# Stationary rows of a transformer kernel: high and low values, and in places the two token halves, stored interleaved

## The chip, the cores and the metric

The kernel runs on one core of one Trainium2 chip. The metric is the device time of one execution in microseconds (us), the median of the runs made. The core's engines are TensorE (in the profile PE for its matmuls and PEld for its weight loads), VectorE (DVE), ScalarE (ACT), GpSimd (POOL) and SyncE (SP, which issues most DMAs).

## What is computed

Two transformer layers on 256 tokens of width 1024, all in float32. The first has a gated delta rule and an HGRN2 mixer, then an MLP; the second has convolutions, then a layer of 16384 experts. The two places that the change touches are the MLP's down product (`y` below) and the product of the expert layer's gated activations with the table `v`:

```python
u = jnp.einsum('btd,df->btf', rms_norm(h, pre_mlp_norm[i]), w_mlp_up[i])
y = jnp.einsum('btf,fd->btd', jnp.square(jax.nn.relu(u)), w_mlp_down[i])
...
u_sel = jnp.take(u, idx, axis=0)
act = jax.nn.gelu(jnp.einsum("chkd,cd->chk", u_sel, xc))
v_sel = jnp.take(v, idx, axis=0)
return jnp.einsum("chk,chkd->cd", act * gates, v_sel)
```

The kernel doesn't gather rows of the experts. It multiplies all tokens with all 16384 rows of `u`, weights the result with a gate matrix that is zero where an expert wasn't picked, and multiplies all of that with all rows of `v`.

## The kernel before

**Precision.** A float32 product is made as three products in the fast format `float32r`: each operand is split into a high part (a copy rounded to float32r, made by ACT) and a low part (the float32 value less its high part, made by DVE), and high times high, low times high and high times low are added up in PSUM.

**Stages.** Weights stream in tiles of 128 partitions x 1024 float32 (512 KB) through `ring`, 4 slots deep. ACT splits off `w_hi` (line 1336), DVE `w_lo` (line 1988; GpSimd does it in the expert stage's first half), each 2 slots deep. The order of work is written out by hand on each engine, with semaphores between them.

There are two ways to use a tile on TensorE. In a column product (`up_block` and `out_block`) the weight tile is stationary and 256 tokens move. In a **row product** (`row_tile`, through `passes` at line 639; `closing_rows` at lines 711 and 716 for the last two tiles of a stage) the tokens are stationary and the weights move: for each of the two token halves `t` and the two column halves `c`, 128 token values per partition are loaded and 512 weight columns are streamed. One tile is 12 such pairs of load and matmul: 4 high times high, 4 low times high, then 4 high times low.

**MLP down product** (some 204 to 378 us, between the up products): four rounds, each of 8 tiles up and 8 tiles down. The stationary rows are `mid_hi` and `mid_lo`, 8 buffers `m` of 256 token values each. ACT writes the high part (`mid_copy`, line 1520), DVE the low one (`mid_low`, line 2270). Of the last round the two last tiles go through `closing_rows`.

**Last expert product** (966 us to the end): 128 blocks `n` of 128 experts. 94 are plain tiles, 92 of them through `row_tile` and the last 2 through `closing_rows`. The other 34 form 17 pairs (`pair_products`, lines 1225, 1226 and 1229): two blocks are multiplied as a 2 x 2 block product in 7 products in place of 8, with sums of weights and sums of rows made by DVE. A pair starts at an even `n`; three of its seven products use rows of `wgt` (one of the even block, two of the odd), and four use `pair_x`. The stationary rows `wgt_hi` and `wgt_lo` have 2 buffers, `j % 2`, written by `wgt_high` (line 1730, and line 1783 in the loop) on ACT and by `wgt_low` (line 2651) on DVE. In this stage DVE also splits the weights and makes the sums and low parts of the pairs (lines 2671 and 2676).

In both places the 256 values of a high or low part lie side by side, tokens 0 to 127 first, so one weight load reads 128 consecutive float32, 512 bytes:

```python
wgt_hi = sb("wgt_hi", [P, 2, T], F32R)
wgt_lo = sb("wgt_lo", [P, 2, T], F32R)
mid_hi, mid_lo = split_area("mid", 8, T)
...
return wgt_hi[:, j % 2, t * P:(t + 1) * P], wgt_lo[:, j % 2, t * P:(t + 1) * P]
```

Two further stationary operands serve the prediction. `open_sums` (line 985) clears four PSUM banks by matmuls of bfloat16 zeros with 512 columns. And in the mixer's output product and the gate product the stationary rows come from `hT`, whose block `k` starts at a multiple of 1088 bytes: `out_lhs` takes block `OUT_ORDER[j]` (4, 5, 6, 7, 0, 1, 2, 3) at byte 1088 k, and `gate_lhs` takes block k at byte 1088 k + 64.

Of the kernel before, what the change touches and what calls it, by code (L numbers as in the profile page):

```python
# [17 lines left out]
NT = T // P  # L18
# [41 lines left out]
PEER_BODY = 4  # L60
# [82 lines left out]
def two_stack_kernel(nc, x_in, pT_in, consts_in, cols_in, rows_in, small_in, wab_in, meta_in,  # L143
                     keys_in, stream_in, out):
    ctx = ExitStack()
    with ctx:
        def sb(name, shape, dt=F32):
            return ctx.enter_context(nc.sbuf_tensor(name, shape, dt))
# [22 lines left out]
        hotg = consts[:, C_TRI + 768:C_TRI + 1792].bitcast(F16).rearrange("p (a i n e) -> p a i n e", a=2, i=2, n=4)  # L171
        part16 = consts[:, C_TRI + 256:C_TRI + 384].bitcast(F16)
        sb("up_to_line", [P, (arena_at - nc.sbuf_base) % 512 // 4])
        wgt_hi = sb("wgt_hi", [P, 2, T], F32R)
        wgt_lo = sb("wgt_lo", [P, 2, T], F32R)
        metaT = sb("metaT", [P, KD, META])
        def groups_until(e):

# [4 lines left out]
        taken = [0]  # L183
# [75 lines left out]

        taken[0] = taken_shared  # L260
        mid = area(2, T)
        mid_hi, mid_lo = split_area("mid", 8, T)
        up = area(2, T)
        post = area(NT, D)
        emb = area(NT, D)
# [313 lines left out]
        def _(pe):  # L579
# [408 lines left out]
            transposes(2)  # L988
            open_sums()

            def mid_lhs(m, t):
                return mid_hi[:, m, t * P:(t + 1) * P], mid_lo[:, m, t * P:(t + 1) * P]

            def up_tile(i, m):

# [218 lines left out]


            def wgt_lhs(j, t):
                return wgt_hi[:, j % 2, t * P:(t + 1) * P], wgt_lo[:, j % 2, t * P:(t + 1) * P]

            def pair_products(k):

                n0, first, last = PAIRS[k], k == 0, k == len(PAIRS) - 1

                def high(b, x, w):

                    nc.tensor.matmul(bank[b][:, :], x[0], w, start=first and b >= 4, stop=False)  # L1225
                    nc.tensor.matmul(bank[b][:, :], x[1], w, start=False, stop=False)  # L1226

                def low(b, x, w):
                    return nc.tensor.matmul(bank[b][:, :], x[0], w, start=False, stop=last and b >= 4)  # L1229

                def rows_part(j, t):
                    o = slice(t * P, (t + 1) * P)
                    return wgt_hi[:, (n0 + j) % 2, o], wgt_lo[:, (n0 + j) % 2, o]
# [45 lines left out]
        def _(act):  # L1279
# [235 lines left out]
            def mlp_round(i, closing):  # L1515

                def mid_copy(m):

                    act.wait_ge(mid_step, i * 8 + m + 1)
                    nc.scalar.activation(mid_hi[:, m, :], mid[:, m % 2, :], ACT.Copy).then_inc(mid_high, 1)  # L1520

                for m in range(8):
                    hi(G_MLP + m + S, i, 16)
# [203 lines left out]

            def wgt_high(j, at):

                nc.scalar.activation(wgt_hi[:, j % 2, :], act_all[:, at, :], ACT.Copy).then_inc(wgt_step, 1)  # L1730

            for e in range(TAIL, N_KEYS):
                gelu_turn(e)
# [45 lines left out]
            with act.Fori(0, V_LOOPED) as i:  # L1779
                for j in range(PEER_BODY):  # L1780
                    hi(G_V + j + S, i, PEER_BODY)
                    act.wait_ge(tiles_done, i * PEER_BODY + (G_V + j + 1))
                    nc.scalar.activation(wgt_hi[:, j % 2, :],
                                         act_all[:, bass.ds(i * PEER_BODY + (j + 2), 1), :].rearrange("p a t -> p (a t)"),
                                         ACT.Copy).then_inc(wgt_step, 1)
            for n in range(V_LOOPED * PEER_BODY + 2, N_KEYS):
                if n in G_OF and n - 2 not in PAIR_OF:
# [165 lines left out]
        def _(dve):  # L1953
# [313 lines left out]
            def mid_low(i, m):  # L2267

                dve.wait_ge(mid_high, i * 8 + (mid_high0 + m + 1))
                nc.vector.tensor_tensor(mid_lo[:, m, :], mid[:, m % 2, :], mid_hi[:, m, :].bitcast(F32),  # L2270
                                        ALU.subtract).then_inc(mid_out, 1)

            def mlp_round(i, closing):
# [374 lines left out]
            def wgt_low(j, at, n):  # L2648

                dve.wait_ge(wgt_step, n + 1)  # L2650
                nc.vector.tensor_tensor(wgt_lo[:, j % 2, :], at, wgt_hi[:, j % 2, :].bitcast(F32), ALU.subtract)\  # L2651
                    .then_inc(wgt_out, 1)

            for e in range(TAIL, N_KEYS):
# [269 lines left out]
```

## Time and profile before

| | before |
|---|---|
| median of 2 runs | 1313.28 us (1312.39 to 1314.16) |
| the profiled execution | 1312.56 us, of which its span 1310.8 us |
| PE busy | 1283.9 us, 98% of the span, 7580 matmuls |
| PEld busy (weight loads) | 1121.9 us, 86% |
| DVE busy | 1029.5 us, 79% |
| ACT busy | 808.8 us, 62% |
| POOL busy | 441.3 us, 34% |
| chain that ended last | PE 84%, DVE 11% |
| row products in that chain (L639 with column products) | 41% of the span |

The chain that ended last is followed back from the last instruction. The end of a matmul in the profile is modelled: a matmul of 512 columns shows as 389 ns, while the next one starts after 227 ns. So the pace of a stream of matmuls is read from the starts, not from the durations; where several are merged in the view in order of time, the distance between two merged rows' starts over the count is their pace.

### The profile page before, as it was taken

What the parts mean: (1) busy time and instruction counts of PE and PEld (TensorE: products, weight loads), DVE (VectorE), ACT (ScalarE), POOL (GpSimd) and SP (SyncE); (2) the same over time, 40 slices, a digit from 0 to 9 for tenths busy, and PEclk for the clock granted to TensorE, in tenths of its full rate; (3) what the DMA queues carried; (4) which work ended last, traced back from release to release, by engine and by line L of the source; (5) the groups of instructions that cost most, each with busy time, mean ns of one, the idle gap of its engine ahead of it and who ended that gap; (6) DMA issues with size and microseconds to landing.
All of it is one profiled execution on the core that took longest, in us unless ns stands there. A gap on an engine that the chain in (4) does not pass through costs nothing.

```text
span 1310.8 us, 22781 instructions
## 1 busy us (share of the span) xinstructions
PE 1283.9 (98%) x7580; PEld 1121.9 (86%) x7580; DVE 1029.5 (79%) x2015; ACT 808.8 (62%) x1553; POOL 441.3 (34%) x255
## 2 busy tenths in 40 slices
PE   7999999999998999999999999999999999999997
PEld 7998988888877997998888888888888888888886
DVE  4787658556666985689996889898746899999996
ACT  6546446445566445455667888888756566666664
POOL 2100415000023754038888777777750000000000
PEclk9999999999999999999999999999999999999999
DMA  8533136565544544545555455444466665655553
GB/s 306 178 113 112 35 97 202 192 192 191 188 163 142 169 131 129 175 162 188 183 185 181 161 162 161 162 162 162 161 196 223 223 203 199 204 197 193 196 190 113
DMA packets 64651, 225.38 MB, mean 172 GB/s; under 512 B 7200, under 2 KB 7712, under 8 KB 64176
## 3 DMA queue, kind: packets, MB, share of 16 engines
q1 hardware_dynamic: 62832, 218.36, 50.6%
q10 hardware_dynamic: 1728, 5.84, 1.3%
q8 instruction: 53, 0.87, 0.3%
q14 instruction: 38, 0.31, 0.1%
HBM read 223.12 MB, written 1.05 MB: 171 GB/s over the span
## 4 chain that ended last, share of the span: by engine, by line
PE 84%; DVE 11%; issue 2%; ACT 1%; DMA 0%; POOL 0%; SPq 0%; POOLq 0%; ACTq 0%; DVEq 0%
PE bank L639 41%; PE bank L654 17%; PE bank L659 9%; PE bank L1198 2%; PE bank L1225 2%; PE bank L1226 2%; PE bank L1229 2%; DVE arena L2521 1%; DVE arena L2524 1%; DVE arena L2523 1%; DVE bank L2503 1%; DVE w_lo L1988 1%; DVE arena L2522 1%; PE bank L755 1%; PE bank L903 1%
## 5 line engine op out<-in xcount | busy, mean ns | idle before, releaser
L1336 ACT ACTIVATE w_hi<-ring 128x1024 fp32r<-128x1024 f32 x380 | 402.1, 1058 | 340.3 <-issue 167.2
L1988 DVE TENSOR_TENSOR w_lo<-ring,w_hi 128x1024 fp32r<-128x1024 f32 x225 | 275.3, 1224 | 141.1 <-ACT w_hi L1336 140.2
L1940 POOL TENSOR_TENSOR w_lo<-ring,w_hi 128x1024 fp32r<-128x1024 f32 x128 | 308.2, 2409 | 142.0 <-ACT w_hi L1336 142.0
L654 PE MATMUL bank<-hT,w_hi 128*128 128x512 f32 x1272 | 324.1, 396 | 1.9 <-ACT arena L1678 1.9
L654 PEld LDWEIGHTS bank<-hT,w_hi 128*128 128x128 f32 x1272 | 228.2, 189 | 43.2 <-ACT arena L1678 2.3
L1837 POOL TENSOR_SCALAR mstat<-mstat 128x1 f32<-128x1 f32 x16 | 5.8, 362 | 536.1 <-ACT bank L1293 334.2
L659 PEld LDWEIGHTS bank<-hT,w_lo 128*128 128x128 f32 x1272 | 173.5, 190 | 12.7
L659 PE MATMUL bank<-hT,w_lo 128*128 128x256 f32 x1272 | 177.1, 282 | 0.0
L639 PE MATMUL bank<-w_hi,wgt_hi 128*128 128x512 f32 x368 | 143.4, 390 | 0.2 <-DVE wgt_lo L2651 0.2
L639 PE MATMUL bank<-w_hi,wgt_lo 128*128 128x512 f32 x368 | 143.2, 389 | 0.0
L639 PE MATMUL bank<-hT,w_hi 128*128 128x256 f32 (+2 forms) x848 | 113.1, 286 | 0.0
L639 PEld LDWEIGHTS bank<-hT,w_hi 128*128 128x128 f32 x848 | 106.1, 189 | 0.6
L639 PE MATMUL bank<-w_lo,wgt_hi 128*128 128x512 f32 x368 | 98.4, 389 | 0.0
L2503 DVE TENSOR_TENSOR bank<-bank,consts 128x256 f32<-128x256 f32 x128 | 55.0, 432 | 48.0 <-ACT consts L1656 40.6
L1730 ACT ACTIVATE wgt_hi<-arena 128x256 fp32r<-128x256 f32 x116 | 47.0, 406 | 63.6 <-PE bank L639 60.5
L639 PEld LDWEIGHTS bank<-w_hi,wgt_hi 128*128 128x128 f32 x368 | 69.1, 188 | 15.2 <-issue 1.0
L1718 ACT ACTIVATE consts<-consts,idxT 128x128 f16<-128x128 f16 x256 | 81.4, 396 | 0.0
L639 PEld LDWEIGHTS bank<-w_lo,wgt_hi 128*128 128x128 f32 x368 | 69.1, 188 | 14.4
L639 PEld LDWEIGHTS bank<-w_hi,wgt_lo 128*128 128x128 f32 x368 | 69.1, 188 | 14.2
L1901 POOL TENSOR_TENSOR w_lo<-ring,w_hi 128x1024 fp32r<-128x1024 f32 x26 | 62.8, 2414 | 25.9 <-ACT w_hi L1336 24.5
L639 PE MATMUL bank<-hT,w_lo 128*128 128x256 f32 (+2 forms) x424 | 59.4, 282 | 0.0
L2651 DVE TENSOR_TENSOR wgt_lo<-arena,wgt_hi 128x256 fp32r<-128x256 f32 x128 | 54.7, 428 | 5.1 <-ACT wgt_hi L1730 5.1
(397 smaller groups left out, 2190.1 us busy)
## 6 DMA issues: line engine op xcount, KB each, us to landing
ring<-in_stream SPq DMA_DIRECT2D x380, 512.0 KB, 3.6
arena<-in_stream SPq DMA_DIRECT2D x34, 512.0 KB, 4.6
arena<-in_rows ACTq DMA_DIRECT2D x1, 1536.0 KB, 11.3
consts<-in_consts ACTq DMA_DIRECT2D x1, 1152.0 KB, 6.8
arena<-in_keys ACTq DMA_DIRECT2D x1, 1024.0 KB, 4.7
h<-in_x SPq DMA_DIRECT2D x2, 256.0 KB, 4.0
h<-in_x ACTq DMA_DIRECT2D x2, 256.0 KB, 3.9
arena<-in_rows ACTq DMA_DIRECT2D x1, 512.0 KB, 4.1
```

The lines of the kernel that those rows point to most:

```text
L639: mm = nc.tensor.matmul(o, a, b, start=first and not low_part and xp is x[0], stop=last and low_part)
L654: mm = nc.tensor.matmul(both, w_hi[:, slot, k * P:(k + 1) * P], x_both[:, k, :, :], start=k == 0, stop=False)
L659: mm = nc.tensor.matmul(bank[b][:, 0:T], w_lo[:, slot, k * P:(k + 1) * P], x_hi[:, k, :], start=False, stop=k == KD - 1)
L1198: mm = nc.tensor.matmul(bank[half][:, n * P:(n + 1) * P], hot2[:, half, n, :], hotg[:, half, i, n, :], start=i == 0, stop=i == 1)
L1336: nc.scalar.activation(w_hi[:, g % S, :], ring[:, g % R, :], ACT.Copy).then_inc(hi_done, 1)
L1718: ins = nc.scalar.activation(hotg[:, s % 2, 0, n, :], hot1[:, n, :], ACT.Copy, scale=idxT[:, 2, 4 * s + n:4 * s + n + 1])
L1730: nc.scalar.activation(wgt_hi[:, j % 2, :], act_all[:, at, :], ACT.Copy).then_inc(wgt_step, 1)
L1901: nc.gpsimd.tensor_tensor(w_lo[:, g % S, :], ring[:, g % R, :], w_hi[:, g % S, :].bitcast(F32), ALU.subtract).then_inc(lo_done, 1)
L1940: nc.gpsimd.tensor_tensor(w_lo[:, g % S, :], ring[:, g % R, :], w_hi[:, g % S, :].bitcast(F32), ALU.subtract).then_inc(lo_done, 1)
L1988: nc.vector.tensor_tensor(w_lo[:, g % S, :], ring[:, g % R, :], w_hi[:, g % S, :].bitcast(F32), ALU.subtract).then_inc(lo_done, 1)
L2503: nc.vector.tensor_tensor(half, half, up_u[:, at % 2, :], ALU.add).then_inc(up_out, 1)
L2651: nc.vector.tensor_tensor(wgt_lo[:, j % 2, :], at, wgt_hi[:, j % 2, :].bitcast(F32), ALU.subtract)\
```

## The change

The high and the low rows of one buffer now share 512 values, in one of five layouts. In each, the load of one part of one token half still reads 128 values; what differs is the step from one to the next. `apart` is the old layout (step 4 bytes). `by_part` interleaves high with low (step 8). `by_token` interleaves the token halves and keeps high and low apart (step 8). `by_all` interleaves both (step 16). `by_two` interleaves two neighbouring buffers as well (step 32).

- `wgt`: even buffer `by_part`, odd buffer `by_all`.
- `mid`: buffers 0 and 1 `by_part`, 2 `by_all`, 3 `by_token`, 4 and 5 `by_two`, 6 and 7 `apart`.

The writes on ACT and DVE get the same step, by the same instructions. No instruction, no wait and no matmul is added, removed or moved on any engine, and the buffers take the same bytes as before.

```diff
-        wgt_hi = sb("wgt_hi", [P, 2, T], F32R)
-        wgt_lo = sb("wgt_lo", [P, 2, T], F32R)
+        wgt_both = sb("wgt_both", [P, 2, 2 * T], F32R)
+        def apart(buf):
+            return [buf[:, n * T:(n + 1) * T].rearrange("p (t n) -> p t n", t=NT) for n in range(2)]
+        def by_part(buf):
+            both = buf.rearrange("p (t n a) -> p a t n", t=NT, a=2)
+            return [both[:, n, :, :] for n in range(2)]
+        def by_token(buf):
+            both = buf.rearrange("p (a n t) -> p a t n", t=NT, a=2)
+            return [both[:, n, :, :] for n in range(2)]
+        def by_all(buf):
+            both = buf.rearrange("p (n t a) -> p a t n", t=NT, a=2)
+            return [both[:, n, :, :] for n in range(2)]
+        def by_two(buf):
+            both = buf.rearrange("p (n m t a) -> p m a t n", m=2, t=NT, a=2)
+            return [[both[:, m, n, :, :] for n in range(2)] for m in range(2)]
+        wgt_parts = [by_part(wgt_both[:, 0, :]), by_all(wgt_both[:, 1, :])]
...
-        mid_hi, mid_lo = split_area("mid", 8, T)
+        mid_both = nc.alloc_sbuf_tensor_at("mid_both", [P, 8, 2 * T], F32R, offset=arena_at + 4 * taken[0])
+        mid_parts = [by_part(mid_both[:, m, :]) for m in range(2)] + [by_all(mid_both[:, 2, :])]
+        mid_parts += [by_token(mid_both[:, 3, :])] + by_two(mid_both[:, 4:6, :].rearrange("p a n -> p (a n)"))
+        mid_parts += [apart(mid_both[:, m, :]) for m in range(6, 8)]
...
-                nc.scalar.activation(wgt_hi[:, j % 2, :], act_all[:, at, :], ACT.Copy).then_inc(wgt_step, 1)
+                nc.scalar.activation(wgt_hi[j % 2], like(act_all[:, at, :]), ACT.Copy).then_inc(wgt_step, 1)
...
-                nc.vector.tensor_tensor(wgt_lo[:, j % 2, :], at, wgt_hi[:, j % 2, :].bitcast(F32), ALU.subtract)\
+                nc.vector.tensor_tensor(wgt_lo[j % 2], like(at), wgt_hi[j % 2].bitcast(F32), ALU.subtract)\
```

## Rows read from the trace of the kernel before

**Rows 1.** Page, parts 1 and 4: busy time by engine, chain by engine
```profile
PE 1283.9 (98%) x7580; PEld 1121.9 (86%) x7580; DVE 1029.5 (79%) x2015; ACT 808.8 (62%) x1553; POOL 441.3 (34%) x255
PE 84%; DVE 11%; issue 2%; ACT 1%; DMA 0%; POOL 0%; SPq 0%; POOLq 0%; ACTq 0%; DVEq 0%
```

**Rows 2.** Windows: us, busy (x instructions) of PE, PEld, DVE, ACT, POOL; clock, DMA
```profile
966.00:1304.00 338.00, 337.62 (x1488) 278.38 (x1486) 292.33 (x403) 206.91 (x295) 3.36 (x4) 1.00 0.58 195
1032.00:1286.00 254.00, 254.00 (x1122) 210.31 (x1122) 233.01 (x323) 161.76 (x227) 0.00 (x0) 1.00 0.58 197
204.00:378.00 174.00, 174.00 (x885) 148.48 (x884) 114.06 (x163) 89.91 (x142) 17.58 (x26) 1.00 0.59 191
```

**Rows 3.** Groups by line and form, PE: count | busy us, mean ns | idle before
```profile
L639 PE MATMUL bank<-w_hi,wgt_hi 128*128 128x512 f32 x368 | 143.4, 390 | 0.2 <-DVE wgt_lo L2651 0.2
L1225 PE MATMUL bank<-pair_w_hi,wgt_hi 128*128 128x512 f32 x34 | 13.2, 389 | 0.0
L1225 PE MATMUL bank<-hT,wgt_hi 128*128 128x512 f32 x17 | 6.6, 389 | 0.0
L711 PE MATMUL bank<-w_hi,wgt_hi 128*128 128x512 f32 x8 | 3.2, 399 | 0.2 <-DVE wgt_lo L2651 0.2
L639 PE MATMUL bank<-w_hi,mid_hi 128*128 128x512 f32 x120 | 46.7, 389 | 0.0
L711 PE MATMUL bank<-w_hi,mid_lo 128*128 128x512 f32 x8 | 3.1, 390 | 0.0
```

**Rows 4.** In order of time, PE, in the last product: start us, us
```profile
1060.62 0.39 PE L639 MATMUL bank<-w_hi,wgt_hi 128*128 128x512 f32 x1
...
1063.34 0.39 PE L1225 MATMUL bank<-pair_w_hi,wgt_hi 128*128 128x512 f32 x1
```

**Rows 5.** In order of time, PE: bfloat16 zeros, 512 columns
```profile
200.31 1.03 PE L985 MATMUL bank<-zeros 128*128 128x512 bf16 x4
```

**Rows 6.** In order of time, PE: stationary rows from hT, tiles j = 4 to 6
```profile
185.27 1.98 PE L639 MATMUL bank<-w_hi,hT 128*128 128x512 f32 x8
...
187.99 2.03 PE L639 MATMUL bank<-w_hi,hT 128*128 128x512 f32 x8
...
190.79 0.63 PE L711 MATMUL bank<-w_hi,hT 128*128 128x512 f32 x2
```

**Rows 7.** In order of time, PEld: float32 weight loads back to back
```profile
570.90 1.64 PEld L1150 LDWEIGHTS bank<-arena 128*128 128x128 f32 x14
572.46 0.53 PEld L654 LDWEIGHTS bank<-hT,w_hi 128*128 128x128 f32 x3
```

**Rows 8.** Groups, DVE: rows of wgt, plain writes, writes with a step
```profile
L2651 DVE TENSOR_TENSOR wgt_lo<-arena,wgt_hi 128x256 fp32r<-128x256 f32 x126 | 52.8, 419 | 5.1 <-ACT wgt_hi L1730 5.1
L2671 DVE TENSOR_TENSOR consts<-consts,arena 128x512 f32<-128x512 f32 x34 | 23.3, 684 | 0.0
L2102 DVE TENSOR_TENSOR arena<-arena x14: 674/684/720, 80.5 to 110.1; 128x512 f32<-128x512 f32 x14
```

**Rows 9.** Groups, ACT, 966 to 1304 us
```profile
L1730 ACT ACTIVATE wgt_hi<-arena 128x256 fp32r<-128x256 f32 x114 | 46.3, 406 | 63.6 <-PE bank L639 60.5 <-PE bank L1229 3.1
```

**Rows 10.** Waits, 1032 to 1286 us: total us, times, longest
```profile
DVE consts L2671 <- DMA arena<-in_stream: 9.5, 15, 1.0
DVE w_lo L1988 <- ACT w_hi L1336: 9.0, 19, 0.5
```

More of the change, by code:

```diff
@@ L173, in two_stack_kernel, with like @@
         sb("up_to_line", [P, (arena_at - nc.sbuf_base) % 512 // 4])
-        wgt_hi = sb("wgt_hi", [P, 2, T], F32R)
-        wgt_lo = sb("wgt_lo", [P, 2, T], F32R)
+        wgt_both = sb("wgt_both", [P, 2, 2 * T], F32R)
[13 more added lines that the diff above has]
+            return [[both[:, m, n, :, :] for n in range(2)] for m in range(2)]
+        def like(a):
+            return a.rearrange("p (t n) -> p t n", t=NT)
+        wgt_parts = [by_part(wgt_both[:, 0, :]), by_all(wgt_both[:, 1, :])]
+        wgt_hi, wgt_lo = [p[0] for p in wgt_parts], [p[1] for p in wgt_parts]
         metaT = sb("metaT", [P, KD, META])
@@ L261, in two_stack_kernel @@
         mid = area(2, T)
-        mid_hi, mid_lo = split_area("mid", 8, T)
+        taken[0] = (taken[0] + 7) // 8 * 8
+        mid_both = nc.alloc_sbuf_tensor_at("mid_both", [P, 8, 2 * T], F32R, offset=arena_at + 4 * taken[0])
+        area(8 * 2 * T)
+        mid_parts = [by_part(mid_both[:, m, :]) for m in range(2)] + [by_all(mid_both[:, 2, :])]
+        mid_parts += [by_token(mid_both[:, 3, :])] + by_two(mid_both[:, 4:6, :].rearrange("p a n -> p (a n)"))
+        mid_parts += [apart(mid_both[:, m, :]) for m in range(6, 8)]
+        mid_hi, mid_lo = [p[0] for p in mid_parts], [p[1] for p in mid_parts]
         up = area(2, T)
@@ L989, in _, with tokens_of @@
             open_sums()
+            def tokens_of(part, t):
+                return part[:, t, :]
             def mid_lhs(m, t):
-                return mid_hi[:, m, t * P:(t + 1) * P], mid_lo[:, m, t * P:(t + 1) * P]
+                return tokens_of(mid_hi[m], t), tokens_of(mid_lo[m], t)
             def up_tile(i, m):
@@ L1216, in wgt_lhs @@
             def wgt_lhs(j, t):
-                return wgt_hi[:, j % 2, t * P:(t + 1) * P], wgt_lo[:, j % 2, t * P:(t + 1) * P]
+                return tokens_of(wgt_hi[j % 2], t), tokens_of(wgt_lo[j % 2], t)
             def pair_products(k):
@@ L1231, in rows_part @@
                 def rows_part(j, t):
-                    o = slice(t * P, (t + 1) * P)
-                    return wgt_hi[:, (n0 + j) % 2, o], wgt_lo[:, (n0 + j) % 2, o]
+                    return tokens_of(wgt_hi[(n0 + j) % 2], t), tokens_of(wgt_lo[(n0 + j) % 2], t)
                 a11, a12, a22 = rows_part(0, 0), rows_part(1, 0), rows_part(1, 1)
@@ L1519, in mid_copy @@
                     act.wait_ge(mid_step, i * 8 + m + 1)
-                    nc.scalar.activation(mid_hi[:, m, :], mid[:, m % 2, :], ACT.Copy).then_inc(mid_high, 1)
+                    nc.scalar.activation(mid_hi[m], like(mid[:, m % 2, :]), ACT.Copy).then_inc(mid_high, 1)
                 for m in range(8):
@@ L1782, in _ @@
                     act.wait_ge(tiles_done, i * PEER_BODY + (G_V + j + 1))
-                    nc.scalar.activation(wgt_hi[:, j % 2, :],
-                                         act_all[:, bass.ds(i * PEER_BODY + (j + 2), 1), :].rearrange("p a t -> p (a t)"),
+                    nc.scalar.activation(wgt_hi[j % 2],
+                                         like(act_all[:, bass.ds(i * PEER_BODY + (j + 2), 1), :].rearrange("p a t -> p (a t)")),
                                          ACT.Copy).then_inc(wgt_step, 1)
@@ L2269, in mid_low @@
                 dve.wait_ge(mid_high, i * 8 + (mid_high0 + m + 1))
-                nc.vector.tensor_tensor(mid_lo[:, m, :], mid[:, m % 2, :], mid_hi[:, m, :].bitcast(F32),
+                nc.vector.tensor_tensor(mid_lo[m], like(mid[:, m % 2, :]), mid_hi[m].bitcast(F32),
                                         ALU.subtract).then_inc(mid_out, 1)
```

## The prediction

> **What bounds the kernel now.** I read the page's busy times and its chain first [rows 1]: TensorE is busy 98% of the span and holds 84% of the chain that ended last. Then the windows over the two stages that the change touches [rows 2]. In the last expert product (966 to 1304 us) PE is busy 337.6 of 338 us, and in the stretch of the MLP (204 to 378 us) 174.0 of 174; the granted clock is 1.00 in both, so the engine is at its 2.4 GHz level. Nothing is waited for in these stages that a faster matmul would not shorten, and nothing covers a slower one. The idle time before the row products is 0.2 us in all [rows 3].
>
> So what counts is the pace at which matmuls follow each other, and that stands in the view in order of time. Twelve matmuls of a plain tile take from 1060.62 to 1063.34 us [rows 4]: 2.72 / 12 = 0.2267 us for 512 columns. Compare the four bfloat16 zero products, also of 512 columns [rows 5]: the merged row is 1.03 us long, and its last matmul shows as 0.38 (the zero matmuls' modelled length is that of the others, 0.38 to 0.39), so the pace is (1.03 - 0.38) / 3 = 0.217. A float32 row product thus loses some 10 ns per matmul against the same number of columns in bfloat16.
>
> Is that loss fixed, or does it depend on where the stationary rows lie? The rows from hT answer it [rows 6]. The tile j = 4 (block 0 of hT, byte 0) takes 187.99 - 185.27 = 2.72 us, or 0.2267 per matmul. The tile j = 5 (block 1, byte 1088) takes 190.79 - 187.99 = 2.80, or 0.2333. Both have the same 12 matmuls, the same moving addresses up to the slot, and PE without a gap. Only the start address of the stationary rows differs, so 6.7 ns of a matmul's pace come from that address. I read it as two streams of reads that get in each other's way: the weight load of the next matmul and the moving columns of this one. The load alone takes (572.46 - 570.90) / 14 = 0.111 us for 128 float32 [rows 7], 512 bytes at 4.6 bytes per ns. The moving stream covers 2048 bytes in 0.217 us, 9.5 bytes per ns. So the faster stream passes over the positions of the slower one again and again, in whatever way memory is divided.
>
> At this point a rule of the Trainium skill speaks against the reading: "SBUF — State Buffer", section "Who interferes with whom", has PE's two read ports independent and PE waiting for nobody. By it the layout of the stationary rows could change nothing, and the sum below would be 0. The difference of 2.72 and 2.80 us in [rows 6] does not agree with it, and I follow the rows; what the rule makes of the time is that of rival 1.
>
> **The change part by part.** Nothing is added, removed or moved. Three things get another step in memory.
>
> (1) The weight loads. Per kind, from [rows 3], and each count times three for the products high-high, low-high, high-low: plain tiles 368 x 3 = 1104 and 8 x 3 = 24 in the closing ones, pairs (34 + 17) x 3 = 153, together 1281 with rows of `wgt`. Of the 94 plain tiles 47 have an even n, so 564 matmuls are on each side; each of the 17 pairs has 3 on the even buffer and 6 on the odd. That gives 615 with a step of 8 bytes and 666 with 16. For `mid`, 120 x 3 + 8 x 3 = 384 matmuls, 12 per buffer and round: buffers 0, 1 and 3 give 144 with a step of 8, buffer 2 gives 48 with 16, buffers 4 and 5 give 96 with 32, and 96 stay as they are. In sum: **759 matmuls with a step of 8 bytes, 714 with 16, 96 with 32**.
>
> No strided stationary load stands in the trace, so the price per matmul is bounded by rows. Gain: at most the whole loss against bfloat16, 10 ns [rows 4, 5]. Loss: the only effect of the stationary address that rows show is 6.7 ns [rows 6]; a larger one can't be excluded, see rival 3. With a step of 8 bytes the load runs through memory at 2 x 4.6 = 9.2 bytes per ns, nearly the pace of the moving stream (9.5). Two streams of the same pace either meet at the start, get out of each other's way once, and then keep their distance, or never meet. So I take the whole 10 ns as gained there: 759 x 0.010 = 7.6 us. With 16 and 32 bytes the load is the faster of the two by 2 and 4 times, and the two pass each other about as often as before; I take 0 there, between the bounds -10 and +6.7 ns, that is between -8.1 and +5.4 us for 810 matmuls.
>
> (2) DVE's writes, and its reads of the high rows. With a step of 8 bytes the trace has such an operation: line 2102 works on every second value at its first level (512 values, 14 instructions over seven levels), at 674 to 720 ns, median 684, and the plain one of 512 values takes 684 [rows 8]. So 0 for the step of 8. For 16 and 32 bytes the lower bound is 0, too; as upper bound I double the part that grows with the size, (684 - 419) / 256 = 1.04 ns per value, 265 ns per instruction. On the odd `wgt` buffers that is 49 of the 98 blocks between 1032 and 1286 us, 13 us. DVE is busy 233 of 254 us there [rows 2] with 21 idle, so even this would still fit. The value taken is 0. If this cover went (all 98 at 265 ns, 26 us against 21), 5 us would show.
>
> (3) ACT's writes. 406 ns for 256 values [rows 9], ACT busy 162 of 254 us. 92 us are idle; its waits are for PE. 0.
>
> What a faster TensorE triggers: in the pair stretch it would gain 10 ns on the even buffer's matmuls. That stretch has 98 blocks, of which 17 pairs; 64 plain blocks, half of them even, give 384 matmuls, and the pairs 51, so 4.4 us. 254 becomes 249.6, and DVE needs 233 of it. Its waits for the pairs' DMA (9.5 us) and for ACT's copy (9.0) [rows 10] are late next, but they shrink rather than grow when the rest comes closer. No new wait.
>
> The sum, against the profiled execution's own time (span 1310.8, 1312.56 with what lies around it): 1312.56 - 7.6 = 1305.0. The median of the two runs is 0.7 above that execution, so I predict **1305.6 us**.
>
> **The rivals.**
>
> 1. *The layout changes nothing* (within 3 us): the 10 ns belong to the format and not to where the rows lie, or what 8 bytes give the others take. For it: `wgt`, which lies aligned, has 0.2267 in tile after tile, and so has block 0 of hT. Against it: block 1 of hT. 1313 us.
> 2. *Every step gains*: any load that isn't the slow one of two streams avoids it. 1569 x 0.010 = 15.7 us: 1297.6. For it speaks nothing more than for the forecast; against it, that at 16 and 32 bytes the paces are far apart again.
> 3. *The loads touch more memory and take it from the moving stream: slower.* If what costs is not the meeting but each piece of memory that a load opens, then the present load of 512 bytes opens 32 pieces of 16 bytes and pays 10 ns for them. A step of 8 opens 64, a step of 16 or 32 opens 128. The extra is 759 x 10 = 7.6 us and 810 x 30 = 24.3 us, together 32: 1345 us. It decides as soon as pieces are 16 bytes; with pieces of 64 bytes (now 8; 16, 32 and 64 pieces) the same 10 ns would scale to more. For it: the loss is there for every float32 load, and 32 bytes of step is wasteful in any memory. Against it: the address effect in [rows 6], which a count of pieces (the same from 0 and from 1088) doesn't explain, and the load's own time, which would have to steal from the moving stream rather than use the time it has (0.111 of 0.227 us). The Trainium skill has such a rule: "SBUF — State Buffer", section "Door 1: The DMA port swizzle", speaks of 16-byte lines that want at least two hits each. By it the step of 8 would be free and 16 and 32 would pay, and no row here has such a load.
> 4. *A small loss*: the steps of 16 and 32 pay the 6.7 ns of [rows 6], and 8 gains nothing: 810 x 0.0067 = 5.4 us, 1319; in between lie mixtures.
>
> **How the numbers follow.** Forecast (3 to 13 us faster) 0.42; every step gains 0.10; nothing 0.20; small loss up to 26 us 0.14; rival 3 at over 26 us 0.13; anything else 0.01. The likeliest gives 1305.6. The low end is that of rival 2, 1313.3 - 15.7 = 1297.6, with the runs' own spread 1296. The high end goes past rival 4 to 1325, which leaves rival 3 and part of the mixtures above it, some 0.16. The likeliest one's own range is 1300 to 1310. A change of 2% (26 us) is about what a measurement of this kernel can tell from none. Faster by that would need 17 ns per changed matmul, more than the 10 there are: 0.01. Slower 0.13, within 2% 0.86.
>
> **What would show it.** In the view in order of time a plain tile with even n should take 12 x 0.217 = 2.60 us, one with odd n 2.72 as before, and mid's buffers 0, 1 and 3 the same 2.60; buffers 6 and 7 stay at 2.72. Rival 3 shows as tiles longer than 2.72 us, most in mid 4 and 5. PEld's mean of 188 ns should stay. DVE's line for the low rows should stay at 419 ns, and ACT's at 406. The prediction is wrong if even tiles are at 2.72 or above, or if odd tiles move by more than 0.08 us either way, or if DVE's writes grow past the 21 us it has.

## The result and the profile after

The changed kernel takes 1328.03 us, median of 2 runs (1327.34 to 1328.72), against 1313.28 before. The ratio is 1.0112, with a 95% interval of 1.0096 to 1.0129: some 14.7 us **slower**, within the 2% band, but on the other side of no change from my forecast of 1305.6 and outside its range. The profiled execution took 1327.34 us with a span of 1325.5 (before 1310.8), so the two traces hold the whole difference.

The page of the changed kernel, parts 1 and 4, in the form of [rows 1]:

```profile
PE 1298.8 (98%) x7580; PEld 1166.4 (88%) x7580; DVE 1046.7 (79%) x2015; ACT 825.6 (62%) x1553; POOL 441.8 (33%) x255
PE 85%; DVE 11%; issue 2%; ACT 1%; DMA 0%; POOL 0%; SPq 0%; POOLq 0%; ACTq 0%; DVEq 0%
```

PE is still 98% busy and still the chain, with the same 7580 matmuls. It is 15 us busier, PEld 45 us, DVE and ACT 17 us each. Where it went, by the windows of the last product from its first matmul to its last, first before, then after (columns as in [rows 2]):

```profile
966.15:1303.62 337.47, 337.10 (x1487) 278.23 (x1485) 291.95 (x403) 206.69 (x295) 3.04 (x3) 1.00 0.58 195
```

```profile
969.13:1318.40 349.27, 348.72 (x1487) 313.85 (x1485) 306.66 (x403) 220.59 (x295) 3.01 (x3) 1.00 0.55 189
```

The same 1487 matmuls take 349.3 us in place of 337.5: 11.8 of the 14.8 us of span. The rest, 3 us, arose by the first of them (969.1 against 966.2 us), in the MLP. The granted clock is 1.00 in both, so nothing of it is the clock.

In order of time, PE, of the changed kernel: plain tiles in the loop of the last product (start us, us). The first row starts an odd tile (step 16), the second an even one (step 8), the third the next odd one; the four merged `w_lo` matmuls of each tile are left out.

```profile
1000.02 2.04 PE L675 MATMUL bank<-w_hi,wgt_both 128*128 128x512 f32 x8
...
1002.84 2.03 PE L675 MATMUL bank<-w_hi,wgt_both 128*128 128x512 f32 x8
...
1005.64 2.04 PE L675 MATMUL bank<-w_hi,wgt_both 128*128 128x512 f32 x8
```

An odd tile takes 1002.84 - 1000.02 = 2.82 us and an even one 1005.64 - 1002.84 = 2.80, where [rows 4] had 2.72 for either. Per matmul that is 0.235 at a step of 16, 0.2333 at 8 and 0.2267 before. The same view of the second MLP round, mid buffers 3 (step 8), 4 and 5 (step 32), 6 and 7 (as before):

```profile
277.34 2.03 PE L675 MATMUL bank<-w_hi,mid_both 128*128 128x512 f32 x8
...
280.14 2.12 PE L675 MATMUL bank<-w_hi,mid_both 128*128 128x512 f32 x8
...
283.07 2.13 PE L675 MATMUL bank<-w_hi,mid_both 128*128 128x512 f32 x8
...
286.00 1.99 PE L675 MATMUL bank<-w_hi,mid_both 128*128 128x512 f32 x8
...
288.74 1.98 PE L675 MATMUL bank<-w_hi,mid_both 128*128 128x512 f32 x8
```

2.80 us at step 8, 2.93 at 32 (0.244 a matmul), 2.74 for buffer 6, which follows a step of 32. With the counts of the prediction: 759 x 6.7 ns + 714 x 8 ns + 96 x 17.5 ns = 5.1 + 5.7 + 1.7 = **12.5 us** in the pace of the row products. What is left of the 14.8 is some 2 us.

The groups of the three instructions that got another step (count: duration in ns, shortest / median / longest):

```profile
L675 PEld LDWEIGHTS bank<-w_hi,wgt_both x736: 193/254/338, 969.0 to 1311.0; 128*128 128x128 f32 x184
```

```profile
L2690 DVE TENSOR_TENSOR wgt_both<-arena,wgt_both x128: 407/604/1495, 954.0 to 1314.2; 128x256 fp32r<-128x256 f32 x128
```

```profile
L1769 ACT ACTIVATE wgt_both<-arena x116: 413/548/676, 953.2 to 1312.7; 128x256 fp32r<-128x256 f32 x116
```

Each group has two halves. The loads show as some 193 ns with a step of 8 and some 310 with 16, where the trace of before had 188; mid's with a step of 32 show as some 330. DVE's write takes some 420 and 635 ns (419 before, [rows 8]), ACT's 434 and 657 (406, [rows 9]).

So two things could have cost the time: the loads, or the writes that PE then waits for. And in the loads the mechanism that I had put forward (two streams that meet) had given the wrong sign.

### The profile page after: what moved, and what is told of

Same layout as the page of the kernel before. It is cut to its first block, busy times and chain, and to the rows that moved or that the text cites. A ratio compares the mean times of both kernels' runs of the same rounds, so it can differ in the third digit from the quotient of the medians.

```text
span 1325.5 us, 22781 instructions
## 1 busy us (share of the span) xinstructions
PE 1298.8 (98%) x7580; PEld 1166.4 (88%) x7580; DVE 1046.7 (79%) x2015; ACT 825.6 (62%) x1553; POOL 441.8 (33%) x255
## 4 chain that ended last, share of the span: by engine, by line
PE 85%; DVE 11%; issue 2%; ACT 1%; DMA 0%; POOL 0%; SPq 0%; POOLq 0%; ACTq 0%; DVEq 0%
PE bank L675 42%; PE bank L690 17%; PE bank L695 9%; PE bank L1238 2%; PE bank L1265 2%; PE bank L1269 2%; PE bank L1266 2%; DVE arena L2560 1%; DVE arena L2563 1%; DVE arena L2562 1%; DVE bank L2542 1%; DVE arena L2561 1%; PE bank L791 1%; PE bank L939 1%; PE bank L925 1%
## 5 line engine op out<-in xcount | busy, mean ns | idle before, releaser
L675 PE MATMUL bank<-w_hi,wgt_both 128*128 128x512 f32 x736 | 188.8, 398 | 0.3 <-ACT w_hi L1375 0.3
L675 PEld LDWEIGHTS bank<-w_hi,wgt_both 128*128 128x128 f32 x736 | 161.3, 253 | 16.5 <-ACT w_hi L1375 0.7
L1769 ACT ACTIVATE wgt_both<-arena 128x256 fp32r<-128x256 f32 x116 | 63.1, 545 | 64.1 <-PE bank L675 61.1
L675 PE MATMUL bank<-w_lo,wgt_both 128*128 128x512 f32 x368 | 101.1, 396 | 0.0
L675 PEld LDWEIGHTS bank<-w_lo,wgt_both 128*128 128x128 f32 x368 | 82.4, 252 | 7.4
L2690 DVE TENSOR_TENSOR wgt_both<-arena,wgt_both 128x256 fp32r<-128x256 f32 x128 | 68.4, 535 | 10.6 <-ACT wgt_both L1769 10.6
L675 PE MATMUL bank<-w_hi,mid_both 128*128 128x512 f32 x240 | 61.3, 397 | 0.0
L675 PEld LDWEIGHTS bank<-w_hi,mid_both 128*128 128x128 f32 x240 | 51.4, 244 | 5.4
## 6 DMA issues: line engine op xcount, KB each, us to landing
arena<-in_rows ACTq DMA_DIRECT2D x1, 1536.0 KB, 11.8
```

The lines of the kernel that those rows point to most:

```text
L675: mm = nc.tensor.matmul(o, a, b, start=first and not low_part and xp is x[0], stop=last and low_part)
L1769: nc.scalar.activation(wgt_hi[j % 2], like(act_all[:, at, :]), ACT.Copy).then_inc(wgt_step, 1)
L2690: nc.vector.tensor_tensor(wgt_lo[j % 2], like(at), wgt_hi[j % 2].bitcast(F32), ALU.subtract)\
```

## The experiments

Times are compared with runs of the kernel before that were made beside them on the same chip: 1314.26 us for the loads and the writes, 1314.05 for the step of 8 and for one engine's writes, 1314.02 for the shifted `w_lo`. The other experiments ran once and are read for their traces only.

### Loads or writes

`r1_loads_only`: ACT and DVE write as before, only the loads take the new steps (the same edit for `mid`, for the pairs and in DVE's writes is left out here).

```diff
+        wgt_rd = wgt_parts
+        wgt_wr = [apart(wgt_both[:, j, :]) for j in range(2)]
...
-                return tokens_of(wgt_hi[j % 2], t), tokens_of(wgt_lo[j % 2], t)
+                return tokens_of(wgt_rd[j % 2][0], t), tokens_of(wgt_rd[j % 2][1], t)
...
-                nc.scalar.activation(wgt_hi[j % 2], like(act_all[:, at, :]), ACT.Copy).then_inc(wgt_step, 1)
+                nc.scalar.activation(wgt_wr[j % 2][0], like(act_all[:, at, :]), ACT.Copy).then_inc(wgt_step, 1)
...
```

> ACT and DVE write the rows side by side as before; only the weight loads read with the steps of the change (so they pick up mixed values, and the output is not the reference's). Theory A (the pace of the row products is what cost: in the changed kernel's trace tiles take 2.80, 2.82 and 2.92 us at steps of 8, 16 and 32 bytes against 2.72): 759 x 6.7 + 714 x 8.0 + 96 x 17 ns = 12.4 us slower than before, about 1326, and no single late tile per pair. Rival W (the doubled writes at a step of 16 bytes, DVE 419 to 620 ns and ACT 406 to 655, make PE wait and so cost most of it): within 4 us of before, about 1315.

Measured: 1326.09 us, ratio 1.0093 (1.0076 to 1.0110), 11.8 us slower. Tiles at 2.80, 2.82 and 2.93 us as in the changed kernel. Theory A, with its 12.4 us, holds; rival W falls as the main cause.

`r2_writes_only`: the same edit with the two roles exchanged (`wgt_rd` apart, `wgt_wr = wgt_parts`).

> The other half: ACT and DVE write with the steps of the change, the loads read 128 consecutive values as before (mixed values, output not the reference's). Theory A: tiles back at 2.72 us, only the late tile once per pair remains (some 0.09 us x 17 and 0.7 us once), 0 to 2.5 us slower than before, about 1315. Rival W: 10 us or more slower.

Measured: 1321.63 us, ratio 1.0060 (1.0043 to 1.0076), **7.4 us** slower. Both theories missed: the writes alone cost three times what I allowed them under A, and less than W wanted. The two halves make 11.8 + 7.4 = 19.2 us, and together they cost 14.7: when the loads slow PE down, most of the writes' cost is hidden again. The trace of this run shows it: tiles that don't wait take 2.72 us, and one tile in each pair's period is late. First the tiles, in order of time on PE:

```profile
1041.49 1.98 PE L679 MATMUL bank<-w_hi,wgt_both 128*128 128x512 f32 x8
...
1044.21 1.98 PE L679 MATMUL bank<-w_hi,wgt_both 128*128 128x512 f32 x8
...
1047.18 2.08 PE L679 MATMUL bank<-w_hi,wgt_both 128*128 128x512 f32 x8
```

2.72 and then 2.97 us. Then all engines around the end of the late one:

```profile
1045.28 1.22 DVE L2031 TENSOR_TENSOR w_lo<-ring,w_hi 128x1024 fp32r<-128x1024 f32 x1
...
1046.42 0.61 DVE L2694 TENSOR_TENSOR wgt_both<-arena,wgt_both 128x256 fp32r<-128x256 f32 x1
...
1047.15 0.53 PEld L679 LDWEIGHTS bank<-w_hi,wgt_both 128*128 128x128 f32 x3 [0.48 <-issue]
```

DVE's low rows for the next tile end at 1046.42 + 0.61 = 1047.03, and PE's first load follows at 1047.15, after 0.48 us without one. With the old 0.42 us the rows would have been there 0.19 us earlier. Of all distances between two matmuls of the last product 43 are over 260 ns and add 7.1 us to the steady pace in this run, against 6 and 1.0 us before. In the changed kernel they are 21 and 2.8 us.

Whose write is it? `r8_dve_16` and `r9_act_16` give the steps to one engine each.

```diff
-        wgt_hi, wgt_lo = [p[0] for p in wgt_parts], [p[1] for p in wgt_parts]
+        wgt_apart = [apart(wgt_both[:, j, :]) for j in range(2)]
+        wgt_hi, wgt_lo = [p[0] for p in wgt_apart], [p[1] for p in wgt_parts]
+        wgt_read = [p[0] for p in wgt_apart]
...
-                return tokens_of(wgt_hi[j % 2], t), tokens_of(wgt_lo[j % 2], t)
+                return tokens_of(wgt_read[j % 2], t), tokens_of(wgt_read[j % 2], t)
...
```

(`r9_act_16` has `wgt_parts` for the high part and `wgt_apart` for the low one, and reads the low one twice. In both, DVE adds the float32 rows to themselves in place of subtracting the high part, so neither computes the reference's values.)

> The change's steps for wgt only in DVE's write of the low rows (odd buffer 16 bytes, 419 to some 620 ns); ACT writes side by side; the loads read the consecutive high values for both parts (output not the reference's); mid as before. All tiles that don't wait should take 2.72 us. If DVE's longer write is what costs in the run with the writes alone (7.4 us): 5 to 8 us slower. If ACT's is: under 2 us.

> The same for ACT's write of the high rows (odd buffer 406 to some 655 ns) alone; DVE writes side by side and reads only the float32 rows. If ACT's longer write is what costs: 5 to 8 us slower. If DVE's is: under 2 us. Both at 3 to 4 us would say that they lie one behind the other on one chain, from ACT's high rows through DVE's low rows to PE.

Measured: DVE's step alone 1316.28 us, ratio 1.0019 (1.0010 to 1.0029), 2.2 us; ACT's alone 1314.35, ratio 1.0001 (0.9991 to 1.0010), nothing. The two together are none of the outcomes that I had named: one engine's longer write costs 2 us or nothing, both together 7. The single distances between matmuls show where. Once per pair, at the tile of the rows above, DVE's step alone makes one distance 296 ns in place of 227, 69 ns late; with both steps two distances are some 472 and 307, together 325 ns late; with ACT's alone none is late there. I read it as a chain (ACT's high rows, then DVE's low rows, then PE) that has nearly enough to spare for one longer write and not for two. For it speaks that between 1032 and 1290 us DVE's low rows wait for ACT's 11 times in the run with both and twice with DVE's step alone; that this wait is what adds the rest is argued, not shown. Writes of mid aren't in these two runs, but the last product alone accounts for 6.7 of the 7.4 us in the run with all writes (344.2 us against 337.5).

### The step of 8 alone

`r7_wgt_8`: mid as before, both `wgt` buffers with a step of 8.

```diff
-        wgt_parts = [by_part(wgt_both[:, 0, :]), by_all(wgt_both[:, 1, :])]
+        wgt_parts = [by_part(wgt_both[:, j, :]) for j in range(2)]
...
```

> Both wgt buffers interleaved with a step of 8 bytes, mid as before. A write with that step costs nothing on DVE (419 ns) and some 20 ns on ACT, so only the loads count. Theory A (0.2333 against 0.2267 us per matmul): 1281 x 6.7 ns = 8.5 us slower than before. Rival (the step of 8 alone is free and the step-16 buffer shifts the phase of the stream for its neighbour): tiles at 2.72 us and under 3 us.

Measured: 1321.34 us, ratio 1.0059 (1.0041 to 1.0076), 7.3 us slower; the last product takes 8.0 us longer, near the 8.5 expected. Every plain tile is at 2.80 us, in order of time on PE:

```profile
1002.28 2.03 PE L673 MATMUL bank<-w_hi,wgt_both 128*128 128x512 f32 x8
...
1005.08 2.03 PE L673 MATMUL bank<-w_hi,wgt_both 128*128 128x512 f32 x8
```

DVE's writes stay at 420 ns, ACT's take 430. The step that I had forecast to gain 10 ns per matmul loses 6.7, with no step of 16 or 32 and no longer write on DVE beside it. The layout changes one thing more, though: the low rows now start 4 bytes after the high ones. The last four matmuls of a tile load the high rows alone, which start at multiples of 512 bytes as before, and are 233 to 234 ns apart like the others. That speaks against the low rows' start as the whole cause, but no run has a step of 8 without a shifted start.

### Where the rows start

`r3_scan_starts` and `r6_scan_starts2`: eight buffers of mid, eight starts, the values side by side.

```diff
+        SHIFTS = (0, 4, 16, 32, 64, 96, 128, 192)
...
+        mid_both = nc.alloc_sbuf_tensor_at("mid_both", [P, 8, 640], F32R, offset=arena_at + 4 * taken[0])
...
+        mid_parts = [apart(mid_both[:, m, SHIFTS[m] // 4:SHIFTS[m] // 4 + 2 * T]) for m in range(8)]
```

> wgt as before. The eight mid buffers hold consecutive values, but start 0, 4, 16, 32, 64, 96, 128 and 192 bytes past a multiple of 512. Theory M (the two read streams meet, and where they start relative to each other counts): the tiles differ from buffer to buffer, 2.72 us at 0, 2.80 at 64, 2.77 to 2.78 at 128 and 2.75 at 192, as the rows of hT did, and writes stay at 400 and 419 ns. Theory P (what counts is how many pieces of 16 bytes a load opens): 32 or 33 pieces in every buffer, so all tiles 2.72 to 2.73.

> wgt as before. The eight mid buffers hold consecutive values and start 256, 160, 208, 224, 240, 248, 252 and 384 bytes past a multiple of 512. Theory M (where load and moving stream stand to each other, with a period of 256 bytes as the rows of hT suggest): 256 bytes like 0 (2.72 us a tile), 384 like 128 (2.79), and the starts between 192 (2.75) and 256 fall from 2.75 to 2.72 or below. If any start is better than 0, it should be one of these, with a tile under 2.72 us. Rival (only a start at a multiple of 256 is good, everything else costs 5 to 7 ns a matmul): 2.79 to 2.81 at all the others.

The tiles of the first, starts 0, 4, 16, (32 left out), 64, 96, 128, 192, in order of time on PE:

```profile
314.81 2.00 PE L675 MATMUL bank<-w_hi,mid_both 128*128 128x512 f32 x8
...
317.56 2.02 PE L675 MATMUL bank<-w_hi,mid_both 128*128 128x512 f32 x8
...
320.35 2.03 PE L675 MATMUL bank<-w_hi,mid_both 128*128 128x512 f32 x8
...
325.95 2.02 PE L675 MATMUL bank<-w_hi,mid_both 128*128 128x512 f32 x8
...
328.73 2.03 PE L675 MATMUL bank<-w_hi,mid_both 128*128 128x512 f32 x8
...
331.54 2.02 PE L675 MATMUL bank<-w_hi,mid_both 128*128 128x512 f32 x8
...
334.33 1.99 PE L675 MATMUL bank<-w_hi,mid_both 128*128 128x512 f32 x8
```

2.75 us for start 0 (the first tile after another stage; its last matmuls are 0.2267 apart), 2.79 for 4, 2.80 for 16 and 32, 2.78 for 64, 2.81 for 96, 2.79 for 128 and 2.75 to 2.76 for 192. Four bytes are enough to lose nearly all that a step of 8 loses. Theory P (pieces of 16 bytes, so no difference) falls. M holds as far as the start counts; that two streams meet is more than these tiles show. The second run closes the circle. Its starts 240, 248, 252 and 384:

```profile
281.24 1.99 PE L675 MATMUL bank<-w_hi,mid_both 128*128 128x512 f32 x8
...
283.98 2.03 PE L675 MATMUL bank<-w_hi,mid_both 128*128 128x512 f32 x8
...
286.78 1.98 PE L675 MATMUL bank<-w_hi,mid_both 128*128 128x512 f32 x8
...
289.51 2.03 PE L675 MATMUL bank<-w_hi,mid_both 128*128 128x512 f32 x8
```

2.74 to 2.75 us, 2.80, 2.73 and 2.79; 160, 208 and 224 gave 2.78 to 2.80. So 384 is like 128, and 256 was like 0, as a period of 256 bytes wants (two pairs, and 2.79 is what many other starts give, too). But between 192 and 256 the tile doesn't fall steadily, as I had expected: 240 and 252 are good, 248 isn't. No start beat 2.72.

### How long a load takes by itself

`r4_scan_steps`: mid buffers with steps of 12, 20, 32, 36, 48, 64, 96 and 24 bytes.

```diff
+        STEPS = (3, 5, 8, 9, 12, 16, 24, 6)
...
+            both = buf.rearrange("p (n s) -> p s n", s=q)
+            return [both[:, a:a + 3:2, :] for a in range(2)]
...
```

> wgt as before. The eight mid buffers are read and written with steps of 12, 20, 32, 36, 48, 64, 96 and 24 bytes. Theory L (from a step of 16 bytes the load itself, 310 ns in the trace against 188, takes so long that it sets the pace): every step of 20 and more gives the same tile, 2.82 to 2.93 us, loads all 310 to 330 ns; 12 bytes (two of four loads open a new piece) between 2.80 and 2.82. Theory P (pieces of 16 bytes, 128 from a step of 16 up): the same flat line at 2.82. Theory M (streams meet by where they are): the tile goes up and down with the step, and 64 and 96 bytes, which come back to few places, are the worst, over 2.95. Writes: ACT about 650 and DVE about 620 ns from 16 bytes up, about 500 at 12.

`r5_load_alone`: such buffers again, with steps of 4, 8, 16, 32, 48, 64, 96 and 24 bytes (not shown in the diff), and with only 64 columns streamed per load.

```diff
-                    row_tile((s, i * 16 + (G_MLP + 8 + m + 1)), lambda t: mid_lhs(m, t), 0, False, False)
+                    passes((s, i * 16 + (G_MLP + 8 + m + 1)),
+                           [(bank[2 * t + c][:, 0:64], mid_lhs(m, t), slice(c * HALF, c * HALF + 64), False, False, False)
+                            for t in range(NT) for c in range(2)])
```

> wgt as before. The mid buffers are read with steps of 4, 8, 16, 32, 48, 64, 96 and 24 bytes, and the matmuls of the MLP's down product stream only 64 of their 512 columns (the other columns are left out), so that hardly anything else reads while a load runs; the last two tiles of the last round stream all 512. Theory L (the load's own length sets the pace from a step of 16 bytes up): the pace alone is about the one seen with 512 columns, 0.235 us at 16, 0.244 at 32, 0.268 at 48, and not below. Theory M (both streams slow each other where they meet): alone, all steps from 16 up have one and the same pace, near twice the 0.112 us of consecutive values, 0.215 to 0.23, and the differences between 16, 32, 48, 64 and 96 bytes are gone; 4 and 8 bytes at 0.112.

With 512 columns (the first run), the tiles at steps of 36, 48, 64, 96 and 24 bytes, in order of time on PE:

```profile
325.92 2.12 PE L689 MATMUL bank<-w_hi,mid_a 128*128 128x512 f32 x8
...
328.85 2.33 PE L689 MATMUL bank<-w_hi,mid_a 128*128 128x512 f32 x8
...
332.06 2.05 PE L689 MATMUL bank<-w_hi,mid_a 128*128 128x512 f32 x8
...
334.89 2.17 PE L689 MATMUL bank<-w_hi,mid_b 128*128 128x512 f32 x8
...
337.92 2.04 PE L689 MATMUL bank<-w_hi,mid_b 128*128 128x512 f32 x8
```

With 64 columns (the second run), steps of 16, 32, 48, 64, 96 and 24:

```profile
316.02 2.05 PE L689 MATMUL bank<-w_hi,mid_a 128*128 128x64 f32 x8
...
318.82 2.10 PE L689 MATMUL bank<-w_hi,mid_a 128*128 128x64 f32 x8
...
321.69 2.32 PE L689 MATMUL bank<-w_hi,mid_a 128*128 128x64 f32 x8
...
324.89 1.93 PE L689 MATMUL bank<-w_hi,mid_a 128*128 128x64 f32 x8
...
327.51 2.20 PE L689 MATMUL bank<-w_hi,mid_b 128*128 128x64 f32 x8
...
330.53 1.97 PE L689 MATMUL bank<-w_hi,mid_b 128*128 128x64 f32 x8
```

Side by side, us per tile of 12 matmuls. Most are the rows' distances; the last tiles, and those with 64 columns at 4 and 8 bytes, are read from the starts of the single matmuls, and 1.34 is 12 x 112 ns. With 512 columns, 4 to 16 bytes are from the runs above.

| step, bytes | 4 | 8 | 16 | 24 | 32 | 48 | 64 | 96 |
|---|---|---|---|---|---|---|---|---|
| 64 columns | 1.34 | 1.41 | 2.80 | 2.68 | 2.87 | 3.20 | 2.62 | 3.02 |
| 512 columns | 2.72 | 2.80 | 2.82 | 2.82 | 2.95 | 3.21 | 2.83 | 3.03 |

Steps of 12, 20 and 36 bytes gave 2.87, 2.86 and 2.93 us with 512 columns. (At 12 one distance of 287 ns, the tile's first, is part of it.)

This separates two regimes. At steps of 16, 32, 48 and 96 bytes the tile with nearly nothing to stream is as long as the tile with everything, to 0.08 us: **the load itself sets the pace**, and the matmul waits for its weights. Theory L holds there, and M, which wanted one and the same load at all these steps, falls. I had expected of L that it would be flat, and it isn't: a load of 128 float32 takes 219 ns at 64 bytes and 267 at 48. At steps of 4 and 8 the load needs 112 and 118 ns and is far from being the bound; what 8 costs, 6.7 ns, looks like what a shifted start costs. At 24 and 64 bytes (2.68 and 2.62 alone, 2.82 and 2.83 together) the load is just below the 227 ns of a matmul, and the two together take 8 to 9 ns more than that; how much of that is the load's isn't shown. In all these layouts from 16 bytes up the four loads of a buffer also start 0, 4, 8 and 12 bytes in, so step and start weren't taken apart.

### With 256 columns, and an attempt to use it

`r10_256_columns` and `r12_256_starts`: the edit of the run above with 256 in place of 64 columns, and starts in place of steps (the second 256 columns of each product are left out in both, in the second one too).

> wgt as before. The matmuls of the MLP's down product stream 256 of their 512 columns (the others are left out; the last two tiles of the last round stream all 512). Buffers 0 to 4 hold consecutive values with starts of 0, 4, 16, 64 and 96 bytes, buffer 5 has a step of 8, buffer 6 one of 16, buffer 7 is as buffer 0. Theory M (the loss is made where a load runs beside a moving stream, once per load): the same 6 to 7 ns per matmul over buffer 0 at starts of 4 to 96 and at a step of 8, on a pace of 0.120 instead of 0.227, so 0.126. Rival K (the loss grows with the columns streamed, so it sits in the moving stream alone): half, 3 ns, 0.123. Step 16 has the pace of its load alone in either case, 0.233, and not half of that.

> wgt as before. Row products of the MLP with 256 columns, mid buffers of consecutive values starting 64, 32, 48, 80, 128, 160, 192 and 224 bytes past a multiple of 512. Theory S: 0.1135 us per matmul at 64 again, now in the first place of the eight; the rest between 0.113 and 0.120, each a number of its own. Rival: 64 at 0.118 to 0.120 here, so its place in the round made it.

The tiles of starts 0 and 4 in the first, in order of time on PE:

```profile
259.87 1.12 PE L676 MATMUL bank<-w_hi,mid_both 128*128 128x256 f32 x8
...
261.30 1.11 PE L676 MATMUL bank<-w_hi,mid_both 128*128 128x256 f32 x8
...
262.72 1.10 PE L676 MATMUL bank<-w_hi,mid_both 128*128 128x256 f32 x8
```

1.43 and 1.42 us, or 0.120 and 0.118 us a matmul. The step of 8 has 0.119 to 0.120, the step of 16 has 0.233 to 0.234, as alone. So with 256 columns neither a start of 4 nor a step of 8 costs anything; at a start of 4 a matmul is even 2 ns faster. M's 6 to 7 ns per load and K's half of it both fall: what an unfavourable place costs depends on the columns too, and not in proportion. Several later tiles of these two runs had PE waiting for `w_hi` and `w_lo`, which are split as fast as before for half the work, so I read only their undisturbed matmuls. The 0.1135 us at a start of 64 in the first run was such a tile; the second run, with 64 in the first place, had 0.118.

`r11_w_lo_64` tried to use the 0.1135 us of the first run, which the second had not yet put right: the kernel before, with `w_lo` moved by 64 bytes.

```diff
+        sb("ahead_of_w_lo", [P, 16])
         w_lo = sb("w_lo", [P, S, D], F32R)
+        sb("behind_w_lo", [P, 112])
```

> The kernel before with one edit: w_lo starts 64 bytes later (16 unused float32 ahead of it, 112 behind, so that everything after it keeps its place up to a multiple of 512 bytes). In the run with 256 columns a stationary start of 64 bytes had matmuls 0.1135 us apart, against 0.120 at 0. The column products with w_lo stationary and 256 tokens moving (line 659, 1272 matmuls) have just that form and are 0.120 apart. Theory S (the start of the stationary rows relative to the moving ones sets the pace, for any pair of buffers): line 659 at 0.1135, 1272 x 6.5 ns = 8.3 us gained; in the row products w_lo moves, so the stationary rows stand 64 bytes before it, as at a start of 192: +2.7 ns on some 650 matmuls, 1.8 us lost; in sum 6 to 7 us faster than before, about 1307.5. Rival (the 0.1135 came from ACT or DVE holding that tile up, or holds for the mid buffers' place alone): line 659 stays at 0.119 to 0.120 and the kernel is within 2 us of before.

Measured: 1319.31 us, ratio 1.0044 (1.0031 to 1.0058), 5.3 us slower. The column products with `w_lo` stationary went from 0.120 to 0.118 us a matmul, 2 ns and not 6.5. The row products lost more than expected. A down tile of the MLP in this run, from its first matmul to the next tile's:

```profile
272.80 0.39 PE L641 MATMUL bank<-w_hi,mid_hi 128*128 128x512 f32 x1
...
275.58 0.39 PE L641 MATMUL bank<-w_hi,mid_hi 128*128 128x512 f32 x1
```

2.78 us against 2.72, though only 4 of its 12 matmuls stream `w_lo`: the matmuls of `w_hi` that follow those start at distances of 231, 236, 228, 232, 231 ns and come back to 227 only at the sixth. The four of `w_lo` are 236, 235, 232 and 232 ns apart. So the good pace of a stream takes several matmuls to settle, and such a tile changes its stream twice.

A change of place isn't the only thing that starts this. In the kernel before, the column products of the expert layer alternate between 8 matmuls of 512 columns (line 654) and 8 of 256 (line 659), with both operands at multiples of 512 bytes from the start of the first buffer. In order of time, PE, of the kernel before:

```profile
600.51 2.00 PE L654 MATMUL bank<-hT,w_hi 128*128 128x512 f32 x8
602.35 1.12 PE L659 MATMUL bank<-hT,w_lo 128*128 128x256 f32 x8
603.30 2.00 PE L654 MATMUL bank<-hT,w_hi 128*128 128x512 f32 x8
```

The 8 of line 654 take 1.84 us in place of 8 x 0.2267 = 1.81: their distances are 234, 235, 229, 232, 231 and then 227, 226, 227 ns, nearly the row of numbers that follows `w_lo` above. So the four distances of `w_lo` may be this settling alone, and the run doesn't show what the place of the moving rows costs a settled stream.

No version that does all of the kernel's work beats the kernel before.

## Why the prediction was wrong

- **What bounds the kernel: right.** PE is the chain in both traces, at the same clock, and some 12.5 of the 14.8 us are matmuls that follow each other more slowly. Nothing covered them.
- **That the place of the stationary rows counts: right.** [rows 6] read as they were: 0.2333 us at an unaligned start, and the starts of the two scans other than 0, 252 and 256 give 0.229 to 0.234.
- **The step of 8 bytes as a gain of 10 ns: wrong, and this is the step that failed.** It came out at -6.7 ns, 759 times: 5.1 us lost in place of 7.6 gained. The argument was that two streams of equal pace (9.2 and 9.5 bytes per ns) meet once and then keep their distance. The paces were nearly equal, as assumed: at a step of 8 the load takes 118 ns (8.7 bytes per ns), and 2048 bytes in 0.2267 us are 9.0. The gain wasn't there all the same. It was a picture with one row behind it, and I let it choose the sign. The row showed only a loss, 6.7 ns, and that is just what the step of 8 cost: [rows 6] was the price itself, not a sign that there was something to gain. The 10 ns against bfloat16 [rows 5] were an upper bound from another format, and no place of the rows in 16 starts and 11 steps gave any of them back.
- **The steps of 16 and 32 as 0: wrong.** I put both at 0 because the streams would pass each other as often as before. I had the load's own 0.111 us [rows 7] and saw that 0.227 us were there for it, but didn't ask how long it would take with another step. At 16 bytes it needs 233 ns by itself and at 32 bytes 240, just over the 227 that it had. That is 6.6 and 13 ns of the 8 and 17.5 ns per matmul that were measured; the rest comes only with the columns streamed beside it. The Trainium skill, "SBUF — State Buffer", section "Door 1: The DMA port swizzle", has lines of 16 bytes, of which a stream wants two hits each. The trace agrees as far as that goes: 118 ns at two values per 16 bytes, 233 at one, against 112 at four. What it would not give is 267 ns at 48 bytes and 219 at 64. I had read this rule as a price to the moving stream (rival 3, 32 us) and not as a price to the load, which hides most of it.
- **DVE's writes: the size was bounded well, the cover wasn't.** I allowed up to 265 ns more at a step of 16; it was 216 (635 against 419), and 254 on ACT. But I let 13 us disappear in 21 us of DVE's idle time over the whole stretch. Idle time elsewhere in the order doesn't help the instruction on which the next tile waits: with the writes alone, 43 distances between matmuls were long and 7.4 us were lost. In the changed kernel only some 2 us of that came through (21 long distances, 2.8 us against 1.0 before); its tiles are 0.08 to 0.10 us longer, which gives the writes that much more time.
- **ACT's writes at 0: right by itself** (1.0001), wrong together with DVE's.
- **The rivals.** None of the four has the right mechanism for all of it. Rival 4 (a small loss) is the nearest: I gave it 0.14 and priced it at 5.4 us, with the 6.7 ns on the steps of 16 and 32 and nothing on the 8. The 8 alone cost 5.1 us, and the steps of 16 and 32 cost 7.4. Had I priced every changed matmul by the one row that I had, 1569 x 6.7 ns = 10.5 us, the forecast would have been 1324, inside my range and 4 us short.
- **The Trainium skill's rule on ports** ("SBUF — State Buffer", section "Who interferes with whom": two independent read ports, PE waits for nobody) gave 0 for the layout by my reading, and the runs don't agree with that: with nothing changed but the start of the rows by 4 bytes, tiles go from 2.72 to 2.79 us. Whether the two streams slow each other or the start costs one of them alone isn't shown; no run has shifted starts with hardly anything streamed.

## What to carry to other kernels

Where one row shows what a change of kind costs, take that row as the price, sign and all, before an argument on how the hardware might work turns it round. A stride in a stationary operand has two prices: the load's own length, to be held against the pace of the matmuls beside it, and, with 512 columns, some 7 ns wherever the rows aren't where the stream runs best. And idle time of an engine covers a longer instruction only if it lies between that instruction and whoever waits for it; here two engines' writes together cost 7 us where one alone cost 2 or nothing.

## What the runs showed of the hardware

- Weight loads of 128 float32 with hardly anything streamed beside them (64 columns; distance from one matmul to the next): 112 ns at a step of 4 bytes, 118 at 8, 233 at 16, 224 at 24, 240 at 32, 267 at 48, 219 at 64, 251 at 96. Not monotone, and nothing here says why.
- Writes of 256 float32r values: DVE 419 ns at 4, 420 at 8, 635 at 16 bytes (622 where its inputs had no step); ACT 403, 430 and 657. At a step of 96 bytes (`r4_scan_steps`) DVE took 793 and ACT 822.
- A float32r row product with 512 columns follows the one before after 0.2267 us only if its stationary rows start at 0, 256 or 252 bytes past a multiple of 512 (of the 16 starts tried), and after 0.229 to 0.234 elsewhere. With 256 columns 0 isn't the best: 0.120 there, 0.118 at 4 and 64. Two pairs of starts fit a period of 256 bytes; what makes the pattern stays open. Whether the start of the moving rows counts by itself or only against the stationary ones wasn't tried apart.
- After a change of stream (other columns, other places) a 512-column stream with aligned operands needs five matmuls of 228 to 236 ns before it is back at 227.
